# A wait on the landing of the third gather back, put in front of every gather of the second expert table

## The reference, cut to what matters

```python
u = jnp.take(u_tab, ic, axis=0)            # first table: (tokens, 8, 16, 1024)
a = jnp.einsum('chkd,cd->chk', u, xc)      # one dot product per token and expert
wgt = gc * jax.nn.gelu(a)
vv = jnp.take(v_tab, ic, axis=0)           # second table
return jnp.einsum('chk,chkd->cd', wgt, vv) # weighted sum of the second table's rows
```

## Time and profile before

| what | value |
|---|---|
| median of three runs | 1311.55 us (1310.23 to 1312.46) |
| the profiled execution's own time: its span | 1366.9 us |
| busy: PE, DVE, POOL, ACT | 1199.9, 861.8, 500.2, 420.2 us |
| gathers, queue q0 | 273.19 MB with the few others on it, 53.1% of 16 engines' span |
| loads by SP, queue q1 | 127.48 MB, 25.8% |
| gathers of either table on POOL | 256 + 256, 957 and 947 ns each |
| dot products on DVE (L2489) | 256, 1217 ns each |

### The profile page before, as it was taken

The page is one execution under the profiler, slowest core; times in us unless marked ns, Lnnn a source line. Parts: engine busy times, 40 slices in busy tenths (PEclk is TensorE's granted clock), DMA queues, the critical chain, the costliest instruction groups (busy, mean ns, idle before and its releaser), DMA issues. The chain is left out here.

```text
span 1366.9 us, 14592 instructions
## 1 busy us (share of the span) xinstructions
PE 1199.9 (88%) x4663; PEld 665.4 (49%) x4663; DVE 861.8 (63%) x1765; ACT 420.2 (31%) x1138; POOL 500.2 (37%) x580
## 2 busy tenths in 40 slices
PE   7899888888778978876788889789999999999997
PEld 4676554433344542222345433236544545999443
DVE  2657669574663654776746557679989543676345
ACT  2213334344223343343423324432323311222000
POOL 1000356666665666766666666630000000000000
PEclk9999999999998999999999999999999999999999
DMA  9998789999998999999999999986644444454450
GB/s 358 390 349 326 286 319 339 367 357 367 364 366 300 406 403 405 407 377 364 340 371 353 400 405 409 377 306 233 224 139 148 145 150 156 157 175 145 175 184 31
DMA packets 134303, 405.66 MB, mean 297 GB/s; under 512 B 10153, under 2 KB 11585, under 8 KB 133971
## 3 DMA queue, kind: packets, MB, share of 16 engines
q0 software_dynamic: 75024, 273.19, 53.1%
q1 hardware_dynamic: 57860, 127.48, 25.8%
q10 hardware_dynamic: 1342, 4.06, 0.8%
HBM read 403.12 MB, written 1.05 MB: 296 GB/s over the span
## 5 line engine op out<-in xcount | busy, mean ns | idle before, releaser
L1143 PE MATMUL psum<-gathered,modr 128*128 128x512 f32 x1024 | 505.0, 633 | 130.3 <-DMA gathered<-in_peer_v_dram,expert_idx 49.0
L2489 DVE CUSTOM_DVE_ANT_0 gathered<-gathered,psum 128x1024 f32<-128x1024 f32 x256 | 311.5, 1217 | 202.3 <-DMA gathered<-in_peer_u_dram,expert_idx 153.3
L1143 PEld LDWEIGHTS psum<-gathered,modr 128*128 128x128 f32 x1024 | 190.7, 199 | 404.7 <-issue 284.9
L687 POOL DMA_INDIRECT gathered<-in_peer_u_dram,expert_idx x256 | 244.9, 957 | 240.5 <-DVE expert_idx L1997 144.0
L701 POOL DMA_INDIRECT gathered<-in_peer_v_dram,expert_idx x256 | 242.6, 947 | 169.9 <-remote 73.7
L780 PE MATMUL psum<-featT,weight_ring 128*128 128x128 f32 (+2 forms) x960 | 145.3, 305 | 14.4 <-issue 11.3
L780 PEld LDWEIGHTS psum<-featT,weight_ring 128*128 128x128 f32 x960 | 133.7, 196 | 43.9 <-issue 35.6
L780 PE MATMUL psum<-weight_ring,featT 128*128 128x512 f32 x336 | 147.9, 596 | 1.3 <-ACT featT L1563 0.8
L1737 ACT ACTIVATE gel<-dots 128x1 f32<-128x1 f32 x256 | 51.1, 200 | 255.1 <-issue 128.1
L1746 ACT ACTIVATE modr<-ident,wgt 128x128 f32<-128x128 f32 x256 | 102.8, 402 | 18.5 <-issue 1.1
L780 PEld LDWEIGHTS psum<-weight_ring,featT 128*128 128x128 f32 x336 | 62.6, 190 | 78.8 <-issue 76.6
(11 more groups left out here) (443 smaller groups left out, 1343.1 us busy)
## 6 DMA issues: line engine op xcount, KB each, us to landing
weight_ring<-in_w_in_dram SPq DMA_DIRECT2D x16, 2048.0 KB
weight_ring<-in_w_up_dram SPq DMA_DIRECT2D x8, 2048.0 KB
weight_ring<-in_w_down_dram SPq DMA_DIRECT2D x8, 2048.0 KB
weight_ring<-in_ada_w_dram SPq DMA_DIRECT2D x5, 2048.0 KB
work<-in_ada_w_dram SPq DMA_DIRECT2D x5, 2048.0 KB, 16.3
weight_ring<-in_peer_wq_dram SPq DMA_DIRECT2D x3, 2048.0 KB
gathered<-in_ada_w_dram SPq DMA_DIRECT2D x2, 2048.0 KB, 14.5
gathered<-in_peer_u_dram,expert_idx POOLq DMA_INDIRECT x256
```

What stands on the lines that cost most here:

```text
L687: pool.indirect_dma_start(u_rows[:, slot, :], None, T["peer_u"], bass.IndirectOffsetOnAxis(ap=expert_idx[:, r % 2, k:k + 1], axis=0),).the ...
L1143: mm = pe.matmul(psum[:, SUM_BANK + half, :], diag[:, e % 8, :], v_rows[:, slot, 512 * half:512 * (half + 1)], start=(e % EXPERTS == 0), s ...
L2489: dve.tensor_tensor_reduce(u_rows[:, slot, :], u_rows[:, slot, :], h2_rows[t], 1.0, 0.0, ALU.mult, ALU.add, dots[:, col:col + 1])
```

## The change

One wait is added to `gather_v`. From the fourth expert on, v(e) also waits until the gather of expert e - 3 of the same table has landed, all 16 parts of it. No instruction is taken away or moved, and the order of the gathers is the same.

```diff
                 r, k, slot = e // ROUTE, e % ROUTE, e % NV
                 if e >= NV:
                     pool.wait_ge(flag("pair_summed"), pairs(e - NV + 1))
+                if e >= 3:
+                    pool.wait_ge(v_full[(e - 3) % NV], 16 * ((e - 3) // NV + 1))
                 if e == 0:
                     turn_wait(pool, "m", 1, 0)
```

## The result

The kernel after takes 1314.06 us (median of 15 runs, 1311.97 to 1316.03); the kernel before took 1311.86 in the 15 runs beside it (1310.23 to 1312.54). The ratio is 1.002, with a 95% interval of 1.0013 to 1.0027: some 2.2 us longer, just inside the 2.6 us that were called no change. That is more than twice the +1 us at which the forecast's sum ended, and just above the forecast's own range of 1310 to 1314 us; the wide range, 1304 to 1325 us, holds it.

The account below looks back on a forecast made before the run. The prediction took DMA byte transfer in the expert stage as the bound, POOL nearly matched. Satisfied waits 0, binding waits 0 to +1 us and stalls 0 summed to 0 to +1 us on 1311.55: about 1312 us, range 1304 to 1325.

Parts of the forecast that it names:

- A satisfied wait costs 0: On 253 second-table gathers, one more semaphore already satisfied adds 0; 58 us if each cost a second pause.
- How often it binds: Expert stage: binds for about 71 second-table gathers, 440 to 560 and 750 to 840 us of the first profile.
- the case that the 55 us lay there: If the profile's extra 55 us were gaps in the expert stage, runs take 705 us at 401 GB/s, binding nearly throughout.
- the rival by which the wait does next to nothing: Expert stage: queue never over six in unprofiled runs, all waits satisfied on arrival, 1311.55 us; chance 0.12.
- A later issue is not a later landing: Backlogged expert stage: a gather issued later finds a shorter queue and lands at the same time; 0 for transfer rate.
- The spare work at a release: When v(e) is released: five gathers, 6.4 us, remain; POOL needs 1.24 us to add the next; 0 to +1 us.
- The sum that the prediction made by that rule: At a release, 2.0 us beside the bytes leaves 3.4 gathers, 4.4 us of work, against POOL's 1.24 us; still 0.
- "A deep queue looks like a store. It is none.": TensorE or VectorE stalls: slots limit POOL either way, gathers wait on POOL instead of in the queue; 0.
- the prediction's own signs of being wrong: DMA share under 1.0 in 440 to 560 us, POOL pauses over 0.30 us after long-landed third predecessors, or a shorter stage.
- The slower rival: Expert stage: queue runs dry, rate falls to 379 GB/s; +14 us (1326) in bound stretches, +41 (1353) throughout; chance 0.25.
- The faster rival: Mixed stretches with weights: backlog itself costs, shorter queue gives 409 GB/s; 2.5 to 14 us saved, about 1305; chance 0.13.

Follow-up runs that it names:

- seven back: Kernel after with the added wait on the gather seven experts back, always met: 1312.1 us, ratio to before 1.0002.
- the long profile: First profile of the unchanged kernel before: span 1366.9 us, 55 us longer than the runs; a second profile of it had 1310.3 us.
- the first try: 12 POOL additions with drains before v(120), v(212), v(228), added to both kernels: before 1349.16 us (1.0279), after 1352.75 us (1.0316).
- The second try: Holds: four tiny POOL transfers before v(120), v(212), v(228), added to both kernels: before 1314.65 us (1.0022), after 1321.18 us (1.0061).
- Two back: Kernel after with the added wait on the gather two experts back instead of three: 1453.33 us, ratio to before 1.1081.
- the wait from 128 on: Kernel after with the added wait for experts 128 to 255 only: 1313.88 us, ratio 1.0009, beside 1312.29 us of the kernel before.
- the wait up to 127: Kernel after with the added wait for experts 3 to 127 only: 1312.45 us, ratio 1.0005, beside 1312.29 us of the kernel before.
- four back: Kernel after with the added wait on the gather four experts back instead of three: 1311.67 us, ratio to before 0.9999.

## Why the prediction was right, and where it was not

- **A satisfied wait costs 0.** Right: seven back, 1312.1 us.
- **How often it binds.** The stretches 440 to 560 and 750 to 840 us, 71 gathers, were named for the long profile, and nearly the whole stage for the case that the 55 us lay there. The second came true: 704 us at 401 GB/s, a queue of 11.0 us before and 7.0 after. Of the 253 gathers with the wait 183 start within 0.80 us of the landing that they wait for, and no more than seven gathers are under way at once (before: ten), so the rival by which the wait does next to nothing is out.
- **A later issue is not a later landing.** Right for the steady course: from 440 to 520 and 520 to 560 us the kernel after moves 404 and 407 GB/s (before: 405 and 410), and both kernels land an expert every 2.56 us.
- **The spare work at a release.** This is the mis-sized term. The prediction took five gathers, 6.4 us, as left and asked 1.24 us of POOL, which would leave 5.2 us to spare. Measured on purpose at expert 120, a start 1.9 us late moved the landings by 1.2; by itself at 579 us a start 2.4 us late, in a gather 0.6 us longer, moved them by 2.0. So 0.7 to 1.0 us were spare. One part of the gap is POOL's answer to a landing, 0.76 us where 0.30 was taken. Another is time in which a gather is under way but gives the engines nothing to do: v(120), issued into an empty queue in the first try, needed 3.3 us from the end of its issue to its last landing, and its bytes take 1.28, which leaves 3.3 - 1.28 = 2.0 us. The Trainium skill, "DMA: Bandwidth & Descriptors", section "Anatomy of one DMA — SWDGE (gpsimd) path", gives some 2.0 us for that fixed part; the trace agrees. The sum that the prediction made by that rule, 4.4 us left, was nearer than its own, though still too large. With answer, issue and fixed part taken off, 6.4 - 0.76 - 0.94 - 2.0 = 2.7 us should be spare; where the other 1.7 to 2.0 us go is not shown.
- **"A deep queue looks like a store. It is none."** This step failed. It weighed stalls of TensorE and VectorE, which the slots limit in any case, and forgot that POOL itself can be late. The second try shows the store at work: v(228) 3.2 us late in both kernels, nothing lost at 9 to 10 us of depth, 2.4 us lost at 6 (counted from the end of the issue; the 11.0 and 7.0 above are counted from its start). One of the prediction's own signs of being wrong did show: POOL's pause of 2.77 us in front of v(156), whose third predecessor had landed 3.20 us before its start. That the wrong step cost only 2.2 us is luck: POOL was late by more than the spare at few moments of this program.
- **The slower rival** had the right place, the slowest of the 16 engines and what is left for it at a release, and a wrong form: not a rate that falls throughout, but single moments. Two back it is the rate, and the price is 141 us, not 41. **The faster rival**, that the backlog itself costs, is refuted in its own stretch: from 440 to 520 us the kernel after, with the shorter queue, moves 404 GB/s and the kernel before 405.

What is open: the loss at v(57), around 304 us (390 GB/s in the tenth slice), is a second moment of the same kind; by v(88) the kernel after is 1.4 us behind. At v(104) it is level again, 441.56 against 441.55 us. Most of that comes in one step: v(101) lands 3.53 us behind v(100) in the kernel before and 2.54 in the kernel after; why was not found. Nor was the cause of POOL's pause in front of v(156). It is in the profiles of three back, four back and the wait from 128 on, and not in those of the kernel before, of the wait up to 127 and of either kernel with holds. So the added wait may have a part in bringing the pause as well as in laying it bare; that was not tested. Letting v(e) go when half of the 16 parts of v(e-3) have landed, which would part the slowest engine from POOL's answer, was not tried.

## What to carry to other kernels

Count a queue's depth in time, not in transfers: take off the answer of the engine that refills it and the part of each transfer that moves no bytes, and what is left is at most how late the refilling engine may be, once, before it shows. Here that sum gives 2.7 us, and 0.7 to 1.0 were measured, so measure it by a hold of known length. At a steady rate a queue can look full, with 400 GB/s and a DMA share over 1, and still have a spare of only 1 us; look for single slices in which the rate drops, and see what the issuing engine did just before. The landing that counts is that of the slowest of the 16 engines, so a dip in the mean rate (351 GB/s over 24 us, four back) costs nothing as long as that one has work.

## What the runs showed of the hardware that was not expected

- An addition on POOL with a drain behind it, issued behind indirect gathers, was followed by a standstill that ended 1.4 to 3.5 us after all of them had landed: at expert 120 13.40 us with the deep queue, 7.50 with the short one, and some 12 us of the kernel's time for each. Which of the two brings it was not separated. Small transfers issued at the same place took 0.50 us each and did not wait.
- The 16 DMA engines do not keep step: with a deep queue the parts of one gather of 512 KB land over 6.3 us, and the last part comes 3.4 us behind the third last. With ever shorter queues the parts land within 3.9, 2.3 and 1.5 us.
